# First modulation matrix in two column halves, with the first products of two strips between them, and the bias passes in parts

## The chip, the core and the metric

The kernel runs on one NeuronCore of a Trainium2 chip. The metric is device time in microseconds (us) for one execution of the whole program. The kernel before has a median of 1760.36 us over 3 runs (1759.49 to 1760.89).

## What is computed

A transformer stack on 256 tokens of width 1024: two layers of one kind, then two of another, all in float32. What the change touches is the first thing the first layer does: a modulation vector out of the condition, a modulated RMS norm, and a gated feed-forward block (FFN) of inner width 2816. The relative-position bias of the window attention, which comes later, is prepared in the same opening.

```
cond = silu(c)
mod = cond @ w_mod[l] + b_mod[l]            # 9 vectors of 1024: sh1, sc1, g1, ...
h = modulate(x, norm_g[l, 0], sh1, sc1)     # rms_norm(x) * g * (1 + sc1) + sh1
x = x + 0.5 * g1 * swiglu(h, w_ffn1_gu[l], w_ffn1_down[l])
...
bias[h, q, k] = rel_bias[bucket(pos_q - pos_k), h]   # window attention, masked where k > q
```

Each float32 product is made of three products in a reduced format: a "hi" part and a "lo" remainder of both operands, as hi*hi + lo*hi + hi*lo.

## The kernel before

**Weights.** A weight unit is 128 x 1024 float32, 512 KB. SyncE's queue loads units into a ring of 6 (`raw`); ScalarE makes the hi part of a unit (`hi_static`, L810), VectorE the lo part (`lo_static`, L1355), both into rings of 7. The queue reloads a ring slot when the lo part is done (`lo_done`). The first FFN has 11 strips of 256 inner columns. A strip is four gate/up units and two down units. The first three strips (0, 1, 2) have the tokens as the stationary operand (`gate_up`, `strip_unit`); from strip 3 on the weights are stationary (`turned_unit`). The gate/up sums of strip 0 lie in PSUM banks 2 and 3, those of strips 1 and 2 in banks 4 and 5 (`gu_banks`).

**The opening.** The first two modulation vectors, sh1 and sc1, are needed before any product can be made. Their matrix, 1024 x 2048, is loaded as 16 units (m0 to m15; m0 to m7 are all rows of the sc1 columns, m8 to m15 those of the sh1 columns) through SyncE's queue, into 4 arena tiles and the 6 ring slots, some of them twice (`mod_load` then waits for `mod_read`). TensorE multiplies each by the condition (`mod_unit`, L2222). VectorE turns the result into columns, `mod_store` (L1388 to L1390), the scale first and the shift in two pieces. Between the units TensorE makes four of the six bias passes (`bias_pass`, L2235, 16 small matmuls of 72 columns each) and transposes the normed x (`x_turn`, L2279). VectorE makes what a bias pass reads (`bias_reach`, L1397, 128 x 2048) and takes its result (`bias_take`, L1405, four reductions).

**Splitting x.** The transposed x comes as 8 groups: 4 pairs of 128-column chunks for each of 2 token halves. ScalarE and VectorE scale and shift them (`x_scaled`, L851 and L1472); ScalarE writes the hi part (`x_hi`, L860), VectorE the lo part (`x_low`, L1483). `opening_strip` (L2293, L2298) makes the products of strip 0, one unit at a time, each with two groups. Then comes the loop over strips: strip 1 with bias passes 4 and 5 in it, strip 2, and so on. After strip 0, VectorE computes `silu(gate) * up` in `gated` (L1679), TensorE transposes the product (`turn`, L2386), and the two are split for the down units.

**VectorE's modulation units.** All later modulation vectors are computed on VectorE (`mod_unit` there, L1368, one pass of 128 x 1024 each), from tiles that GpSimd's queue loads. In the first FFN there are 48, five or six for each strip from strip 2 on. VectorE's order in a turned strip is written out by hand: lo parts, modulation units, `half_sum` (L1690), lo parts, `half_made`, `half_lo`, and so on.

**The order** of the instructions of every engine is thus fixed in the text of the kernel; engines meet at semaphores. An engine that waits holds up all that stands behind it in its own order.

## Time and profile before

| | |
|---|---|
| median of 3 runs | 1760.36 us |
| profiled execution, its own time | 1760.84 us |
| its span in the trace | 1759.0 us |
| TensorE busy | 1733.1 us (99%) |
| VectorE busy | 1418.9 us (81%) |
| ScalarE busy | 1006.6 us (57%) |
| GpSimd busy | 186.0 us (11%) |
| HBM read | 438.38 MB, 250 GB/s over the span |

The span is 1.8 us shorter than the execution's own time, and that execution is 0.5 us above the median. Times in the rows are microseconds from the span's start. PE is TensorE, PEld its weight load, DVE VectorE, ACT ScalarE, POOL GpSimd, SP SyncE; a q behind the name is the engine's own sequencer. L with a number is a line of the kernel before. A float32 matmul that is not split shows as two instructions, so that one modulation unit on TensorE is x8.

### The profile page before, as it was taken

To read this page: it belongs to the slowest core of one execution; us is meant where nothing else is said; L and a number is where in the kernel's file an instruction comes from. 1 tells how busy PE (TensorE), PEld (TensorE's weight loads), DVE (VectorE), ACT (ScalarE), POOL (GpSimd) and SP (SyncE) were. 2 spreads that over 40 slices of the span, in tenths; PEclk is the share of its full clock that TensorE was granted. 3 is DMA by queue.
4 is the path that set the end of the run, shared out by engine and by line. 5 is a ranking of instruction groups with operands and counts; after the bars stand their busy time and mean duration, and the time that the engine had idled before them with its cause. 6 is when DMAs were issued, how large, how long until landed. Compare 5 with 4: busy or idle time off the path is not lost.

```text
span 1759.0 us, 24722 instructions
## 1 busy us (share of the span) xinstructions
PE 1733.1 (99%) x9178; PEld 1471.9 (84%) x9178; DVE 1418.9 (81%) x2185; ACT 1006.6 (57%) x1666; POOL 186.0 (11%) x382
## 2 busy tenths in 40 slices
PE   6999999999999999999999999999999999999998
PEld 3888888888888888988888888888888888888886
DVE  7899987898899888879888866579888876688565
ACT  4545577755475556877555644556455544465454
POOL 3021012111111111021110000001110000010000
PEclk9999999999999999999999999999999999999999
DMA  9999742698859985418898554458886484566551
GB/s 342 367 348 394 283 139 91 254 341 329 319 220 341 324 324 208 168 51 320 330 336 288 225 206 156 161 191 335 322 328 247 171 297 149 186 221 251 204 195 69
DMA packets 125144, 441.10 MB, mean 251 GB/s; under 512 B 15248, under 2 KB 18272, under 8 KB 124896
## 3 DMA queue, kind: packets, MB, share of 16 engines
q1 hardware_dynamic: 91024, 316.17, 48.9%
q0 software_dynamic: 33296, 120.12, 18.2%
q10 hardware_dynamic: 704, 3.23, 0.5%
q8 instruction: 73, 1.20, 0.3%
q14 instruction: 47, 0.39, 0.1%
HBM read 438.38 MB, written 1.09 MB: 250 GB/s over the span
## 4 chain that ended last, share of the span: by engine, by line
PE 95%; DVE 2%; DMA 1%; ACT 1%; issue 0%; SPq 0%; DVEq 0%; ACTq 0%
PE banks L2366 24%; PE banks L2167 15%; PE banks L2371 12%; PE banks L2145 12%; PE banks L2172 7%; PE banks L2150 6%; PE banks L2315 2%; PE banks L2319 2%; PE banks L2324 2%; PE banks L2135 1%; PE banks L2137 1%; PE banks L2136 1%; DMA weights_raw<-in_w_mod_first 1%; PE banks L2279 1%; PE banks L2604 1%; DVE weights_lo L1355 1%
## 5 line engine op out<-in xcount | busy, mean ns | idle before, releaser
L1355 DVE TENSOR_TENSOR weights_lo<-weights_raw,weights_hi 128x1024 fp32r<-128x1024 f32 (+2 forms) x584 | 685.7, 1200 | 67.8 <-ACT weights_hi L810 66.9
L810 ACT ACTIVATE weights_hi<-weights_raw 128x1024 fp32r<-128x1024 f32 (+2 forms) x584 | 584.5, 1035 | 69.3 <-DMA weights_raw<-in_w_in 22.0
L2366 PE MATMUL banks<-hT,weights_hi 128*128 128x512 f32 x1856 | 464.1, 392 | 0.0
L2366 PEld LDWEIGHTS banks<-hT,weights_hi 128*128 128x128 f32 x1856 | 337.3, 189 | 63.0
L2371 PEld LDWEIGHTS banks<-hT,weights_lo 128*128 128x128 f32 x1856 | 253.2, 190 | 18.1
L1368 DVE CUSTOM_DVE_ANT_0 arena<-arena,mod_acc,vectors 128x1024 f32<-128x1024 f32 x216 | 267.6, 1279 | 0.0
L2371 PE MATMUL banks<-hT,weights_lo 128*128 128x256 f32 x1856 | 258.8, 282 | 0.0
L1004 ACT ACTIVATE arena<-banks 128x512 f32<-128x512 f32 x116 | 69.5, 599 | 322.7 <-PE banks L2371 322.4
L2145 PE MATMUL banks<-weights_hi,hT 128*128 128x512 f32 (+2 forms) x896 | 218.2, 385 | 0.0
L2145 PEld LDWEIGHTS banks<-weights_hi,hT 128*128 128x128 f32 x896 | 165.6, 188 | 29.9
L1690 DVE TENSOR_TENSOR arena<-banks,arena 128x512 f32<-128x512 f32 x116 | 79.7, 687 | 109.0 <-ACT arena L1004 109.0
L2167 PE MATMUL banks<-weights_hi,actT_hi 128*128 128x512 f32 x520 | 140.7, 392 | 0.0
L2167 PE MATMUL banks<-weights_hi,actT_lo 128*128 128x512 f32 x520 | 139.3, 390 | 0.0
L2172 PE MATMUL banks<-weights_lo,actT_hi 128*128 128x512 f32 x520 | 139.0, 389 | 0.0
L2150 PE MATMUL banks<-weights_lo,hT 128*128 128x512 f32 (+2 forms) x448 | 116.9, 383 | 0.0
L2167 PEld LDWEIGHTS banks<-weights_hi,actT_lo 128*128 128x128 f32 x520 | 97.6, 188 | 21.1
L2172 PEld LDWEIGHTS banks<-weights_lo,actT_hi 128*128 128x128 f32 x520 | 97.6, 188 | 20.2
L2167 PEld LDWEIGHTS banks<-weights_hi,actT_hi 128*128 128x128 f32 x520 | 93.6, 189 | 16.2
L531 POOL DMA_DIRECT2D arena<-in_w_mod x128 | 67.7, 531 | 364.2 <-DVE mod_cols L1368 360.7
L2150 PEld LDWEIGHTS banks<-weights_lo,hT 128*128 128x128 f32 x448 | 83.7, 188 | 15.1
L1009 ACT ACTIVATE arena<-arena 128x256 f32<-128x256 f32 x116 | 48.1, 414 | 75.0 <-DVE arena L1690 74.8
L792 POOL TENSOR_TENSOR x<-x,arena 128x512 f32<-128x512 f32 x10 | 12.8, 1276 | 672.6 <-DVE arena L1513 672.6
(358 smaller groups left out, 1977.8 us busy)
## 6 DMA issues: line engine op xcount, KB each, us to landing
weights_raw<-in_w_ffn_gu SPq DMA_DIRECT2D x176, 512.0 KB, 4.8
arena<-in_w_mod POOLq DMA_DIRECT2D x128, 512.0 KB, 6.2
weights_raw<-in_w_in SPq DMA_DIRECT2D x104, 512.0 KB, 4.2
weights_raw<-in_w_ffn_down SPq DMA_DIRECT2D x88, 512.0 KB, 5.0
arena<-in_w_ada POOLq DMA_DIRECT2D x88, 512.0 KB, 5.6
weights_raw<-in_w_ffn_in SPq DMA_DIRECT2D x88, 512.0 KB, 4.1
weights_raw<-in_w_ffn_out SPq DMA_DIRECT2D x44, 512.0 KB, 4.3
weights_raw<-in_w_out SPq DMA_DIRECT2D x32, 512.0 KB, 3.9
```

Source lines behind the costliest of these rows:

```text
L531: eng.dma_start(mod_tile(m), mod_rows(m)).then_inc(S(mod_sem(m)), 16)
L810: nc.scalar.activation(whi[:, n % PARTS, 0:width], raw[:, slot, 0:width], ACT.Copy).then_inc(S("hi_done"), credit(n))
L1004: nc.scalar.activation(cross_t[:, j], half_banks(j)[:, :, 256:512], ACT.Copy).then_inc(S("half_by_act"), 1)
L1355: V.tensor_tensor(wlo[:, n % PARTS, 0:width], raw[:, n % RING, 0:width], whi[:, n % PARTS, 0:width].bitcast(F32), ALU.subtract).then_inc(S ...
L1368: V.tensor_tensor_reduce(modw[m % MOD_RING], modw[m % MOD_RING], cond_row, 1.0, vec[:, m:m + 1], ALU.mult, ALU.add, modc[:, m:m + 1])\
L1690: V.tensor_tensor(sum_t[:, j], half_banks(j)[:, :, 0:256], cross_t[:, j], ALU.add).then_inc(S("half_by_dve"), 1)
L2145: T.matmul(bank[banks[t]][:, 0:width], src[:, 2 * u + k, P * t:P * (t + 1)], whi[:, slot, k * width:(k + 1) * width], start=u == 0 and k = ...
L2150: ins = T.matmul(bank[banks[t]][:, 0:width], hi_[:, 2 * u + k, P * t:P * (t + 1)], wlo[:, slot, k * width:(k + 1) * width], start=False, s ...
L2167: T.matmul(bank[first_bank + 2 * t + h][:, :], src[:, c, P * t:P * (t + 1)], whi[:, slot, 512 * h:512 * (h + 1)], start=first and i == 0, ...
L2172: ins = T.matmul(bank[first_bank + 2 * t + h][:, :], hi_[:, c, P * t:P * (t + 1)], wlo[:, slot, 512 * h:512 * (h + 1)], start=False, stop= ...
L2366: T.matmul(half_banks(j)[:, kind, :], whi[:, n % PARTS, 256 * k + P * kind:256 * k + P * (kind + 1)], hx[:, :, 4 * q + k, :], start=q == 0 ...
L2371: ins = T.matmul(half_banks(j)[:, kind, 256:512], wlo[:, n % PARTS, 256 * k + P * kind:256 * k + P * (kind + 1)], hhi[:, 4 * q + k, :], st ...
```

## The change

1. **The matrix in halves.** The 16 units are laid out anew: m0 to m7 are all 1024 rows of the first 512 columns of both sh1 and sc1, m8 to m15 the same of the last 512. Every unit has a home of its own (6 ring slots, two tiles of `modacc`, six of `modw`, one arena tile, `gate_b`), so no load waits for a read. Some homes share a semaphore (`FIRST_SEMS`): a reader of m0, m1 or m2 waits for all three, one of m3, m4 or m5 for those three, and m8 with m9, m10 with m11, m12 with m13 in the same way.
2. **The queue.** SyncE's queue now carries m0 to m7, then weight units 0 and 1 (when m0 and m1 are read), m8, m9, unit 2, m10, m11, unit 3, m12 to m15, and units 4 to 7.
3. **The order of products.** The first eight weight units are, as (strip, row group): (0,0), (0,1), (1,0), (1,1), (0,2), (0,3), (1,2), (1,3). The first four need only the first half of the modulation and four of the eight groups of x. m8 to m15 are multiplied between them. The transposes of x come in two lots of 8. `silu` and `gated` of strip 0 come after unit 5 instead of unit 3, its `turn` after unit 6.
4. **`mod_store`** runs once for each half, and makes the scale columns too.
5. **Bias passes.** Three passes (1, 2 and 5) cover only the 64 query rows that are not masked; the other rows of `bias` are set to zero at the start. Passes 0 to 2 stand after m2, m4 and m5; passes 3 to 5 are made in nine parts of 6, 5 and 5 matmuls, in bank 7, between units 5 and 13, each taken by VectorE with one reduction (`bias_take_part`) before the next.
6. **GpSimd's queue** starts its loads for VectorE's modulation units after the hi part of unit 5 instead of unit 3.
7. Three pairs of semaphores are merged into one each (`uq_copied`, `up_copied`, `mix_ready`), with the counts adapted.

The core of the diff:

```diff
-FIRST_RING = 4
+FIRST_SEMS = (0, 0, 0, 3, 3, 3, 6, 7, 8, 8, 10, 10, 12, 12, 14, 15)
+FIRST_UNITS = ((0, 0), (0, 1), (1, 0), (1, 1), (0, 2), (0, 3), (1, 2), (1, 3))
...
-BIAS_AFTER = (2, 4, 8, 9)
-MOD_AHEAD = 12
-X_TURN_AFTER = (8, 12)
+BIAS_AFTER = (2, 4, 5)
+BIAS_ROWS = ((0, P), (64, P), (0, 64), (0, P), (0, P), (64, P))
+REACHED_AT = (0, 1, 0, 2, 3, 2)
+BIAS_PARTS = ((0, 6), (6, 11), (11, 16))
+BIAS_TAKEN = len(BIAS_AFTER) + 3 * len(BIAS_PARTS)
...
+            def first_weights(u):
+
+                b, k = FIRST_UNITS[u]
+                loaded = f"first_w_loaded{u}" if u < PREFETCH else f"w_loaded{u % RING // 2}"
+                if u < RING:
+                    sp.wait_ge(S("mod_read"), u + 1)
+                elif u == RING:
+                    sp.wait_ge(S("lo_done"), RING + 2)
+                sp.dma_start(raw[:, u % RING, :], phases[0][2]["gu"][b, k]).then_inc(S(loaded), 16)
+
+            first_units(0, 8)
+            first_weights(0)
+            first_weights(1)
+            first_units(8, 10)
+            first_weights(2)
+            first_units(10, 12)
+            first_weights(3)
+            first_units(12, 16)
+            for u in range(4, 8):
+                first_weights(u)
...
+                    if f == 0:
+                        pool.wait_ge(S("hi_done"), RING + 6)
...
+            def mod_store(half):
+
+                dve.wait_ge(S("mod_summed"), half + 1)
+                eye = con[:, C_EYE:C_EYE + 32].unsqueeze(1).broadcast_to([P, 8, 32])
+                then(V.tensor_tensor(modm, bank[sum_bank(half)][:, 0:256].rearrange("p (k j) -> p k j", j=32), eye, ALU.mult))
+                then(V.tensor_reduce(modr[:, :], modm, AX, ALU.add))
+                cols = slice(4 * half, 4 * half + 4)
+                at = [w[:, 0:16].rearrange("p (c k) -> p c k", c=2)[:, :, cols] for w in (modc, vec)]
+                then(V.tensor_tensor(at[0], modr[:, :].rearrange("p (c k) -> p c k", c=2), at[1], ALU.add))
+                g = phases[0][2]["g"] + 4 * half
+                V.scalar_tensor_tensor(sclA[:, cols], modc[:, 8 + 4 * half:12 + 4 * half], 1.0, vec[:, g:g + 4], ALU.add, ALU.mult)\
+                    .then_inc(S("mod_stored"), 1)
...
+                r0, r1 = BIAS_ROWS[q]
+                V.tensor_tensor(reached[REACHED_AT[q]][:, :, r0:r1], posf_q[:, q0 + r0:q0 + r1].unsqueeze(1).broadcast_to([P, 16, r1 - r0]),
+                                posf_k[:, kb, c0:c0 + 16].unsqueeze(2).broadcast_to([P, 16, r1 - r0]), ALU.is_ge).then_inc(S("reached"), 1)
...
+            def bias_take_part(i):
+
+                dve.wait_ge(S("bias_summed"), len(BIAS_AFTER) + i + 1)
+                bias_sums(3 + i // 3, 7, *BIAS_PARTS[i % 3]).then_inc(S("bias_taken"), 1)
...
+            x_stats(1, 0)
+            x_scale0(1)
             bias_take(0)
             bias_reach(2)
             bias_take(1)
-            x_stats(1, 0)
-            x_scale0(1)
-            bias_reach(3)
-            bias_take(2)
             x_stats(1, 1)
             x_scale1(1)
-            mod_store(1)
-            scale_cols(phases[0][2])
-            bias_take(3)
-            bias_reach(4)
-            mod_store(0, 0, 2)
+            bias_take(2)
+            scales[0] = 1
+            mod_store(0)
...
                 if phase[0] == 1:
-                    dve.wait_ge(S("mod_stored"), 2)
+                    dve.wait_ge(S("mod_stored"), 1)
                     x_scaled(a, 0, (0,), first=True)
-                    mod_store(0, 2, 8)
-                    dve.wait_ge(S("mod_stored"), 3)
                     x_low(0)
                     lo_static(n0, SLOT)
                     x_scaled(a, 2, first=True)
                     x_low(1)
-                    x_scaled(a, 3, first=True)
+                    x_scaled(a, 3, (0,), first=True)
                     lo_static(n0 + 1, SLOT)
                     x_low(2)
                     x_low(3)
                     lo_static(n0 + 2, SLOT)
+                    bias_reach(3)
+                    lo_static(n0 + 3, SLOT)
+                    mod_store(1)
+                    dve.wait_ge(S("mod_stored"), 2)
+                    x_scaled(a, 4, (0,), first=True)
                     x_low(4)
-                    x_scaled(a, 5, first=True)
-                    lo_static(n0 + 3, SLOT)
+                    x_scaled(a, 6, first=True)
                     x_low(5)
+                    lo_static(n0 + 4, SLOT)
+                    x_scaled(a, 7, (0,), first=True)
                     x_low(6)
                     x_low(7)
+                    lo_static(n0 + 5, SLOT)
                     x_split_done()
...
+                        c = n0 + 4
+                        units(c + 2, c + 3)
+                        bias_reach(4)
+                        gated(0)
+                        bias_take_part(0)
+                        units(c + 3, c + 4)
+                        act_lo(0)
+                        bias_take_part(1)
+                        units(c + 4, c + 6)
+                        bias_take_part(2)
+                        units(c + 6, c + 8)
+                        bias_take_part(3)
+                        gated(1)
+                        c, mods = n0 + 10, mod_slot(f, 2)
+                        dve.wait_ge(S("cond_row_ready"), 1)
+                        units(c + 2, c + 4)
+                        bias_take_part(4)
                         bias_reach(5)
+                        mod_units(mods[0:1])
+                        bias_take_part(5)
+                        mod_units(mods[1:2])
+                        act_lo(1)
+                        bias_take_part(6)
+                        mod_units(mods[2:3])
+                        units(c + 4, c + 5)
+                        bias_take_part(7)
+                        mod_units(mods[3:])
+                        units(c + 5, c + 6)
+                        bias_take_part(8)
                         units(c + 6, c + 8)
+                        gated(2)
+                        bias_mask(0, 3 * P)
...
+            def bias_part(i):
+
+                pe.wait_ge(S("reached"), 4 + i // 3)
+                pe.wait_ge(S("bias_taken"), len(BIAS_AFTER) + i)
+                bias_products(3 + i // 3, 7, *BIAS_PARTS[i % 3]).then_inc(S("bias_summed"), 1)
...
+            def opening_unit(n, banks, u):
+
+                slot = n % PARTS
+                pe.wait_ge(S("hi_done"), n + 1)
+                for src, sem in ((hhi, "hhi_done"), (hlo, "hlo_done")):
+                    for t in range(NT):
+                        pe.wait_ge(S(sem), tr[0] + 2 * u + t + 1)
+                        for c in range(2):
+                            T.matmul(bank[banks[t]][:, :], src[:, 2 * u + c, P * t:P * (t + 1)], whi[:, slot, 512 * c:512 * (c + 1)],
+                                     start=sem == "hhi_done" and u == 0 and c == 0, stop=False)
+                pe.wait_ge(S("lo_done"), n + 1)
+                for t in range(NT):
+                    for c in range(2):
+                        ins = T.matmul(bank[banks[t]][:, :], hhi[:, 2 * u + c, P * t:P * (t + 1)], wlo[:, slot, 512 * c:512 * (c + 1)],
+                                       start=False, stop=u == 3 and c == 1)
+                ins.then_inc(S("mm_done"), 1)
...
+            def opening(n):
+
+                strips = (gu_banks(0), gu_banks(1))
+                for m in range(8):
+                    if m == 7:
+                        x_turn(1, (0, 1), 1)
+                    mod_unit(m)
+                    if m in BIAS_AFTER:
+                        bias_pass(BIAS_AFTER.index(m))
+                    if m == 4:
+                        pe.wait_ge(S("const_loaded"), 16)
+                        x_turn(0, (0, 1), 1)
+                pe.wait_ge(S("bias_taken"), len(BIAS_AFTER))
+                keep_warm(WARM[0])
                 for u in range(4):
-                    slot = (n + u) % PARTS
-                    pe.wait_ge(S("hi_done"), n + u + 1)
-                    for src, sem in ((hhi, "hhi_done"), (hlo, "hlo_done")):
-                        for t in range(NT):
-                            if u == 0 and t == 1:
-                                pe.wait_ge(S("mod_stored"), 3)
-                            pe.wait_ge(S(sem), tr[0] + 2 * u + t + 1)
-                            for c in range(2):
-                                T.matmul(bank[banks[t]][:, :], src[:, 2 * u + c, P * t:P * (t + 1)], whi[:, slot, 512 * c:512 * (c + 1)],
-                                         start=sem == "hhi_done" and u == 0 and c == 0, stop=False)
-                    pe.wait_ge(S("lo_done"), n + u + 1)
-                    for t in range(NT):
-                        for c in range(2):
-                            ins = T.matmul(bank[banks[t]][:, :], hhi[:, 2 * u + c, P * t:P * (t + 1)], wlo[:, slot, 512 * c:512 * (c + 1)],
-                                           start=False, stop=u == 3 and c == 1)
-                    ins.then_inc(S("mm_done"), 1)
-                tr[0] += X_GROUPS
+                    b, k = FIRST_UNITS[u]
+                    opening_unit(n + u, strips[b], k)
+                    if u < 2:
+                        mod_unit(8 + 2 * u)
+                        mod_unit(9 + 2 * u)
+                    if u == 1:
+                        pe.wait_ge(S("scaled_by_dve"), 3)
+                        pe.wait_ge(S("scaled_by_act"), 3)
+                        x_turn(0, (2, 3), 1)
+                        x_turn(1, (2, 3), 1)
+                    if u == 2:
+                        for m in range(12, 16):
+                            mod_unit(m)
...
+                        if b == 1:
+                            for u in range(4, 8):
+                                s, k = FIRST_UNITS[u]
+                                opening_unit(n0 + u, gu_banks(s), k)
+                                if u == 6:
+                                    turn(0)
+                                if u > 4:
+                                    bias_part(u - 5)
+                            tr[0] += X_GROUPS
+                            down(c + 4, 0, 0, 1)
+                            bias_part(3)
+                            down(c + 4, 0, 1, 2)
+                            bias_part(4)
+                            continue
+                        pe.wait_ge(S("act_ready"), rows_made + b)
+                        gate_up(c, 0, 1)
+                        bias_part(5)
+                        gate_up(c, 1, 2)
                         turn(b - 1)
+                        bias_part(6)
                         gate_up(c, 2, 3)
-                        if f == 0 and b == 1:
-                            bias_pass(5)
-                            pe.wait_ge(S("const_loaded"), 32)
+                        bias_part(7)
                         gate_up(c, 3, 4)
-                        if f == 0 and b == 1:
-                            pe.wait_ge(S("bias_taken"), 6)
+                        bias_part(8)
                         down(c + 4, b - 1)
+                        pe.wait_ge(S("bias_taken"), BIAS_TAKEN)
...
-    laid["w_mod_first"] = np.roll(np.asarray(inputs["w_mod"])[0, :, 0:2 * D], D, axis=1)
+    laid["w_mod_first"] = np.asarray(inputs["w_mod"])[0, :, 0:2 * D].reshape(D, 2, 2, 512).transpose(2, 0, 1, 3).reshape(2, D, D)
```

## Rows read from the trace of the kernel before

**Rows 1.** The page: the chain that ended last, shares by engine.
```profile
PE 95%; DVE 2%; DMA 1%; ACT 1%; issue 0%; SPq 0%; DVEq 0%; ACTq 0%
```
**Rows 2.** Stages: busy us of PE, PEld, DVE, ACT, POOL; granted clock; DMA share; GB/s.
```profile
...
34.00:39.00 5.00, 4.55 (x13) 3.25 (x14) 5.00 (x11) 4.14 (x9) 0.00 (x0) 0.66 0.64 241
39.00:82.00 43.00, 43.00 (x222) 35.41 (x221) 37.98 (x51) 23.89 (x37) 6.58 (x12) 1.00 0.96 372
82.00:226.00 144.00, 143.25 (x755) 122.76 (x754) 140.50 (x204) 79.14 (x121) 24.77 (x49) 1.00 0.88 330
226.00:1759.00 1533.00, 1523.55 (x7977) 1300.81 (x7975) 1210.95 (x1865) 887.14 (x1478) 142.32 (x297) 1.00 0.65 238
...
```
**Rows 3.** The chain that ended last, opening: start, length, what.
```profile
...
5.67 14.74 DMA weights_raw<-in_w_mod_first
...
24.67 5.59 DMA weights_raw<-in_w_mod_first
...
```
**Rows 4.** TensorE's instructions in order of time, 0 to 95 us: start, length, what, idle before.
```profile
...
11.29 1.08 PE L2222 MATMUL banks<-arena,silu_cond 128*32 128x256 f32 x8 [0.20 <-DMA arena<-in_w_mod_first]
12.30 1.14 PE L2235 MATMUL banks<-arena 128*128 128x72 bf16 x16
...
25.30 1.50 PE L2222 MATMUL banks<-arena,silu_cond 128*32 128x256 f32 x24
27.08 1.09 PE L2279 MATMUL banks<-con,arena 128*128 128x128 f32 x8 [0.28 <-DVE window_bias L1405]
...
33.87 0.70 PE L2293 MATMUL banks<-weights_hi,hT 128*128 128x512 f32 x2 [1.78 <-ACT hT L860]
35.02 2.82 PE L2293 MATMUL banks<-weights_hi,hT 128*128 128x512 f32 x6 [0.45 <-ACT hT L860]
...
38.98 1.98 PE L2293 MATMUL banks<-weights_hi,hT 128*128 128x512 f32 x8
...
41.70 1.98 PE L2293 MATMUL banks<-weights_hi,hT 128*128 128x512 f32 x8
...
52.59 0.69 PE L2235 MATMUL banks<-arena 128*128 128x72 bf16 x16
53.12 0.63 PE L2386 MATMUL banks<-con,arena 128*128 128x128 f32 x4
...
81.94 1.98 PE L2366 MATMUL banks<-hT,weights_hi 128*128 128x512 f32 x8
...
```
**Rows 5.** VectorE's instructions in order of time, 0 to 226 us.
```profile
...
8.19 4.55 DVE L1397 TENSOR_TENSOR arena<-arena 128x2048 bf16<-128x2048 f32 x2
...
17.22 1.54 DVE L1405 TENSOR_REDUCE window_bias<-banks 128x96 f32<-128x288 f32 x4
...
23.35 0.15 DVE L1452 RECIPROCAL stat<-stat 128x1 f32<-128x1 f32 x1
...
24.07 0.41 DVE L1388 TENSOR_TENSOR arena<-banks,con 128x256 f32<-128x256 f32 x1
...
25.17 0.17 DVE L1603 SCALAR_TENSOR_TENSOR scale_cols<-mod_cols,vectors 128x8 f32<-128x8 f32 x1
...
66.99 1.28 DVE L1368 CUSTOM_DVE_ANT_0 arena<-arena,mod_acc,vectors 128x1024 f32<-128x1024 f32 x1
...
73.63 4.62 DVE L1355 TENSOR_TENSOR weights_lo<-weights_raw,weights_hi 128x1024 fp32r<-128x1024 f32 x4
78.17 0.74 DVE L1679 TENSOR_TENSOR arena<-arena,banks 128x256 f32<-128x256 f32 x2
...
85.98 0.69 DVE L1684 TENSOR_TENSOR actT_lo<-banks,actT_hi 128x512 fp32r<-128x512 f32 x1 [1.13 <-ACT actT_hi L997]
...
211.80 0.69 DVE L1690 TENSOR_TENSOR arena<-banks,arena 128x512 f32<-128x512 f32 x1 [0.20 <-ACT arena L1004]
...
```
**Rows 6.** ScalarE's instructions in order of time, 0 to 95 us.
```profile
...
31.88 1.06 ACT L810 ACTIVATE weights_hi<-weights_raw 128x1024 fp32r<-128x1024 f32 x1 [6.10 <-DMA weights_raw<-in_w_ffn_gu]
32.84 0.44 ACT L851 ACTIVATE arena<-banks,mod_cols,scale_cols 128x128 f32<-128x128 f32 x1
...
```

220 lines of the change are left out of this document (93 added, 127 removed).

## The prediction

> **What bounds the kernel now.** I read the page's chain first: TensorE holds 95% of the chain that ended last [rows 1]. The stages say where it is not busy: from 39 to 82 us it works 43.00 of 43 us, from 82 to 226 us, the rest of the first FFN, 143.25 of 144, and behind that 1523.55 of 1533 [rows 2]. So a microsecond saved in the opening is kept to the end, if no other engine holds it back. The opening's chain is loading: until 20.41 and again until 30.26 us TensorE's work waits for the first modulation matrix [rows 3], and the first product of the FFN starts at 33.87 [rows 4]. The row that matters as much is the other busy engine: VectorE works 140.50 of the 144 us up to the end of the first FFN [rows 2]. It has next to nothing to give, so TensorE can't run away from it there.
>
> My ledger is therefore in three parts: when the first product starts, when TensorE is through with strip 2 (its next instruction starts at 81.94 now [rows 4]), and where VectorE stands at that time (it starts `gated(2)` at 78.17 [rows 5]).
>
> **Step 1: the first product.** m0 to m2 now share a semaphore, so TensorE starts with m2, at 11.29 as now [rows 4]. Three units at the pace of that row (1.01 to the next) end at 14.4, bias pass 0 at 1.14 at 15.5. From here VectorE's order rules. One take is 1.54, of which the next instruction overlaps some 0.08 (four lo parts are 4.62 long and the next starts 4.54 after): 1.46. A reach is half of 4.55, so a half one 1.13; the reciprocal and the scaling of x take 0.72 (23.35 to 24.07) [rows 5]. Take, half reach, take, scaling, take: 15.6 + 1.46 + 1.13 + 1.46 + 0.72 + 1.46 = 21.9. TensorE meanwhile waits with pass 2 for the second take (19.7) and has pass 2, m6, four transposes and m7 left, half a us each: 21.9 as well, 22.1 with its drain. `mod_store` is 24.07 to 25.34, 1.27 [rows 5]: 23.4. ScalarE then needs a scaling and a hi part, 0.44 each by the row of the scaling [rows 6], and I give 0.1 for the crossings: the first product at 24.4, 9.5 us earlier than now. All loads that this needs are in by then: m8, the ninth unit, lands at 20.41 now [rows 3].
>
> **Step 2: TensorE from there to the end of strip 2.** Now it is 81.94 - 33.87 = 48.1 us: 16 weight units at 2.72 (38.98 to 41.70), 43.5; two bias passes at 0.53 (52.59 to 53.12); two turns, 0.4 each; and 2.7 of waiting and slow clock, nearly all in the first unit, which takes 5.11 [rows 4]. After the change it is: the same 43.5 and 0.8; eight modulation units moved behind the first product, at 0.5 (three in 1.50), 4.0; eight transposes, 1.0 [rows 4]; three bias passes instead of two, 1.6, and 0.3 for entering nine parts instead of three passes, an estimate. Then the waits, from the written orders. In unit 0 group 1's hi part comes 1.2 after group 0's (two scalings and a hi part) against 0.45 of products, 0.7; its lo part stands on VectorE behind the lo part of unit 0 (1.13) and two scalings, 0.5 more. At unit 4, ScalarE makes the hi part of the unit only behind groups 4 and 5: m15's product is ready at 38.9, `mod_store` 1.27, then 0.4, 0.35, 0.7, 0.35 and 1.06 [rows 6] give 43.1, and unit 3 is over at 41.5: 1.6. Units 5 and 10 and the end add 0.6. Waits 3.4. The sum is 54.6, the end 79.0: **2.9 us earlier**. Of the 9.5 us, 4.0 and 1.0 are work only moved, 0.8 is bias work, 0.7 more waits.
>
> **Step 3: VectorE.** Its cost falls by three half reaches (3.4 us), but its place is set by TensorE: it can't store the second half before m15's product. That is unit 0 (2.7 and 1.2), m8 and m9 (1.0), unit 1 (2.7), m10 and m11 (1.0), transposes (1.0), unit 2 (2.7), m12 to m15 (2.0) behind 24.4: 38.7, ready at 38.9. Until then VectorE has run dry: its work from 23.4 (four groups, four lo parts, a reach) ends near 33, more than 5 us idle. From 38.9 to `gated(2)` it has: store 1.3; eight passes over groups at a third of a us, 2.6; 14 lo parts at 1.13, 15.9; a reach and a half one, 3.4; two `gated` at 0.66, 1.3; two lo parts of products at 0.6, 1.2; nine parts of takes, 4.4 as three takes; five modulation units at 1.2, 6.0 [rows 5]; and waits of 3.4 (hi parts of groups 4 and 7 and of units 4 and 5, 2.1, and one for a turn like the 1.13 at 85.98). That is 39.5: `gated(2)` at 78.4, against 78.17 now. **VectorE gains nothing in the opening.**
>
> From there both orders are the same. VectorE's idle time in this stage is 144 - 140.5 = 3.5 us [rows 2]. 1.13 at 85.98 is a wait for ScalarE and, through it, for TensorE [rows 5], with 0.3 behind it; some 0.6 more, the 0.20 at 211.80 in it [rows 5], lies where VectorE has caught up with TensorE in the last strips; with TensorE nearly 3 us earlier these 2.0 us vanish. The other 1.5 are hops of the chain that ends the FFN and stay. So VectorE reaches the last strip 1.8 us earlier, and TensorE, 2.9 early from strip 3 on, waits about 1 us for the split of the last strip's product before its last matmuls. In between there is cover: VectorE takes a strip's sums well before TensorE comes back to their banks. The gain that is left: **1.9 us**. Behind the FFN all engines start together, and nothing else changes (the merged semaphores cost nothing: the same two signals, counted in one).
>
> **The clock.** From 34 to 39 us the granted clock is 0.66 [rows 2], part of the stretch at the 1.2 GHz level, after TensorE had waited 1.78 and 0.45 [rows 4]. Ten matmuls there take 35.02 to 38.98, 3.96 where twelve take 2.72 later: 1.7 us lost. The new order has waits of 1.0, 0.7 and 0.5 around unit 0 and 1.6 before unit 4. A fall at unit 0 delays TensorE and VectorE alike: gain 0.4. A fall at unit 4 overlaps waiting: gain about 1. Or none. I take **1.4 us** for the forecast, nearer to the case without, since the waits are shorter than the one before the fall.
>
> The Trainium skill ("TensorE: Matmul & The Clock Gate", section "Part 1: The HAM clock gate") says that the throttled clock is the default state and sustained activity releases it. By that rule the slow pace of the first units (1.01) would last longer when TensorE starts at 11.29 and not before, so that m3, m4 and pass 1 would take twice their time too. Two units and a pass at the slow rows end 0.5 us behind VectorE's half reach: the gain would be 0.5 less, inside the forecast. The recorded clock shows no low level in these first units, so the trace doesn't decide it.
>
> **Rivals.** *VectorE doesn't bind.* If its waits in step 3 are shorter (it only has 3.4 of them), TensorE's 2.9 come through: 1760.36 - 2.9 = 1757.5. If its waits in unit 0 and before unit 4 shrink too, more. For it speaks that the first unit now loses 2.4 with a slow clock in it; against it VectorE's 140.5 of 144. Chance 0.18, a third of it beyond 3.5 us.
> *Slower: the moved waits meet the slow clock twice.* Place: unit 0 and unit 4; price 1.7 and 1.1, with 0.5 in the first units, 3.3 against 1.9: 1761.8. It decides as soon as `gated(2)` starts more than 1.9 us behind 78.4. For it: the waits are written into the order. Chance 0.12.
> *The loads bind anyway, and the change doesn't do what it says.* m15 is now 20th in the queue. From the ninth (20.41) to the 16th (30.26) a unit took 1.41 [rows 3], so it lands at 35.9, before its product's turn at 38.2. With the queue 0.2 slower per unit the cover is gone, and each further 0.1 costs 1.1 us; 0.4 slower and the gain is used up: no change, 1760.4. DMA share is 0.96 from 39 to 82 us [rows 2]: little to spare. Chance 0.08.
> *Forecast* as above: 0.62.
>
> **Numbers.** The sum is made against the profiled execution, whose span of 1759.0 lies 1.8 below its own time 1760.84, itself 0.5 above the median; I take the gain off the median: 1760.36 - 1.4 = 1759.0. The range goes from the first rival with a little more (1757.2) to between no change and the slower one (1761.3); what is beyond is about 0.15. 0.2% is 3.5 us, about what a measurement of this kernel tells from no change: faster than that 0.08 (part of the first rival and an overlooked gain), slower 0.06 (half of the second), the same 0.86.
>
> **What would show it.** First product at 24 to 25; m15's product near 38.5; `gated(2)` within 1 us of 78.2; strip 3 starting near 79; VectorE without its wait at 86; a new wait of about 1 us on TensorE before the last matmuls of the first FFN, near 213. Wrong, if VectorE's place at strip 3 differs from now by over 1.5 us, if TensorE stalls in strips 3 to 9, or if the last stage (1533 us now) changes its length.

## The result and the profile of the changed kernel

The changed kernel is slower: 1762.72 us median of 20 runs (1761.91 to 1764.17) against 1760.49 (1759.49 to 1761.57) of the kernel before in the same runs, ratio 1.0014 [1.0008, 1.002]. I had predicted 1759.0 with a range to 1761.3; the time lies above it, though within the 0.2% that I had called no difference. The profiled execution took 1764.04 us (span 1762.2), 1.3 above its median; the one of before was 0.35 above 1760.49. So the two traces lie 3.2 us apart where the medians lie 2.2.

First the page's chain, then the stages of the changed kernel (columns as in [rows 2]):

```profile
PE 88%; DVE 9%; DMA 1%; ACT 1%; issue 0%; SPq 0%; DVEq 0%; ACTq 0%
```

```profile
34.00:39.00 5.00, 5.00 (x48) 3.71 (x50) 0.00 (x0) 0.00 (x0) 0.00 (x0) 1.00 1.03 420
39.00:82.00 43.00, 39.75 (x218) 30.20 (x207) 36.46 (x53) 22.69 (x35) 5.78 (x11) 1.00 0.78 291
82.00:226.00 144.00, 142.92 (x752) 121.94 (x751) 142.49 (x204) 76.80 (x114) 22.29 (x42) 1.00 0.90 342
226.00:1762.00 1536.00, 1526.28 (x7988) 1302.84 (x7986) 1212.53 (x1869) 889.30 (x1484) 144.94 (x304) 1.00 0.65 237
```

VectorE's share of the chain went from 2 to 9% [rows 1]. There is no slow clock from 34 to 39 us. From 39 to 82 us TensorE, which had no gap there [rows 2], stands still for 3.3 us; from 82 to 226 VectorE has 1.5 us of idle time left where it had 3.5.

TensorE in order of time (start, length, what, idle before):

```profile
24.66 0.71 PE L2363 MATMUL banks<-weights_hi,hT 128*128 128x512 f32 x2 [1.31 <-ACT hT L877]
...
29.82 2.11 PE L2363 MATMUL banks<-weights_hi,hT 128*128 128x512 f32 x8
31.77 1.07 PE L2368 MATMUL banks<-weights_lo,hT 128*128 128x512 f32 x4
32.77 1.07 PE L2284 MATMUL banks<-arena,silu_cond 128*32 128x256 f32 x16
...
43.93 2.14 PE L2363 MATMUL banks<-weights_hi,hT 128*128 128x512 f32 x8 [1.50 <-ACT weights_hi L829]
...
49.84 0.37 PE L2292 MATMUL banks<-arena 128*128 128x72 bf16 x6
50.05 2.09 PE L2363 MATMUL banks<-weights_hi,hT 128*128 128x512 f32 x8
...
52.91 0.60 PE L2473 MATMUL banks<-con,arena 128*128 128x128 f32 x4
...
62.98 2.11 PE L2207 MATMUL banks<-weights_hi,hT 128*128 128x512 f32 x8 [0.22 <-DVE arena L1723]
...
67.52 0.32 PE L2292 MATMUL banks<-arena 128*128 128x72 bf16 x5 [1.53 <-DVE window_bias L1438]
...
83.65 2.06 PE L2453 MATMUL banks<-hT,weights_hi 128*128 128x512 f32 x8
```

The first product comes at 24.66 instead of 33.87 [rows 4], 9.2 us earlier, as forecast (24.4). (In two later traces of the kernel before with a small edit, e4 and e11, it comes at 32.76 and 32.74, where the last unit of the matrix is multiplied 0.8 us earlier; against those the gain is 8.1.) The first product of strip 3 comes at 83.65 instead of 81.94: all of it is used up, and 1.7 more. Two things are to be seen on the way. The waits: 1.50 as forecast, and 1.53 for a bias take, which was not. And the units: 29.82 to 32.77 is 2.95, 50.05 to 52.91 is 2.86, where a unit of the kernel before took 2.72 [rows 4].

And one thing at the end: strip 3's first product waits for the result of `gated(2)` (`pe.wait_ge(S("act_ready"), rows_made + b)`). In the kernel before, `gated(2)` starts 3.8 us ahead of strip 3 and nobody waits. In the changed kernel and in all its versions below strip 3 starts 0.85 or 0.86 us behind the start of `gated(2)`: VectorE sets this start. Here TensorE's own last unit is over at 83.43, so its wait is only 0.2 us.

VectorE, and ScalarE's two waits for loads:

```profile
39.55 0.42 DVE L1414 TENSOR_TENSOR arena<-banks,con 128x256 f32<-128x256 f32 x1 [5.77 <-PE banks L2284]
...
59.38 2.36 DVE L1379 TENSOR_TENSOR weights_lo<-weights_raw,weights_hi 128x1024 fp32r<-128x1024 f32 x2 [1.37 <-ACT weights_hi L829]
...
64.57 2.36 DVE L1379 TENSOR_TENSOR weights_lo<-weights_raw,weights_hi 128x1024 fp32r<-128x1024 f32 x2 [1.65 <-ACT weights_hi L829]
66.84 0.53 DVE L1438 TENSOR_REDUCE window_bias<-banks 128x120 f32<-128x360 f32 x1
67.28 1.22 DVE L1431 TENSOR_TENSOR arena<-arena 128x1024 bf16<-128x1024 f32 x1
...
82.80 0.75 DVE L1723 TENSOR_TENSOR arena<-arena,banks 128x256 f32<-128x256 f32 x2
...
214.25 0.69 DVE L1734 TENSOR_TENSOR arena<-banks,arena 128x512 f32<-128x512 f32 x1 [0.20 <-ACT arena L1023]
```

```profile
58.29 2.01 ACT L829 ACTIVATE weights_hi<-weights_raw 128x1024 fp32r<-128x1024 f32 x2 [2.26 <-DMA weights_raw<-in_w_ffn_gu]
...
63.40 2.01 ACT L829 ACTIVATE weights_hi<-weights_raw 128x1024 fp32r<-128x1024 f32 x2 [2.56 <-DMA weights_raw<-in_w_ffn_gu]
```

`gated(2)` starts at 82.80, 4.6 us later than before [rows 5] and 4.4 later than forecast. The last `half_sum` of the first FFN is at 214.25 against 211.80 [rows 5], 2.45 later. ScalarE's waits for units 10 to 13, and VectorE's behind them, are not new. The trace of the kernel before has them at the same places:

```profile
58.39 2.01 ACT L810 ACTIVATE weights_hi<-weights_raw 128x1024 fp32r<-128x1024 f32 x2 [2.11 <-DMA weights_raw<-in_w_ffn_gu]
...
63.62 2.01 ACT L810 ACTIVATE weights_hi<-weights_raw 128x1024 fp32r<-128x1024 f32 x2 [2.68 <-DMA weights_raw<-in_w_ffn_gu]
```

```profile
64.71 2.36 DVE L1355 TENSOR_TENSOR weights_lo<-weights_raw,weights_hi 128x1024 fp32r<-128x1024 f32 x2 [2.20 <-ACT weights_hi L810]
```

Units 10 to 13 are ready for ScalarE 0.1 to 0.2 us earlier than before, although the first product comes 9.2 us earlier. The loads of these units, for which ScalarE waits at 58.29 and 63.40, share the DMA engines with six modulation loads of GpSimd. The issues of both queues, and the stages from 40 us on:

```profile
47.23 3.13 POOL L535 DMA_DIRECT2D arena<-in_w_mod  x6 [16.21 <-ACT weights_hi L829]
```

```profile
48.20 6.55 SPq L574 DMA_DIRECT2D weights_raw<-in_w_ffn_gu  x4
```

```profile
40.00:44.00 4.00, 2.50 (x12) 1.75 (x10) 2.75 (x9) 3.06 (x7) 0.00 (x0) 1.00 0.58 198
44.00:48.00 4.00, 4.00 (x16) 2.96 (x17) 3.26 (x5) 2.84 (x5) 0.77 (x2) 1.00 0.35 140
...
56.00:60.00 4.00, 4.00 (x28) 3.00 (x27) 2.63 (x4) 1.74 (x3) 0.00 (x0) 1.00 1.04 422
```

The DMA engines are half idle from 40 to 48 us (shares 0.58 and 0.35; in the kernel before 0.94 and 1.00) and then full (1.04 from 56 us), with ten units asked for within 8 us.

### The profile page after: what moved, and what is told of

It is laid out like the page before. It is cut to its first block, busy times and chain, and to the rows that moved or that the text cites. A ratio compares the mean times of both kernels' runs of the same rounds, so it can differ in the third digit from the quotient of the medians.

```text
span 1762.2 us, 24721 instructions
## 1 busy us (share of the span) xinstructions
PE 1733.7 (98%) x9178; PEld 1470.2 (83%) x9178; DVE 1417.0 (80%) x2184; ACT 1005.8 (57%) x1665; POOL 183.1 (10%) x382
## 4 chain that ended last, share of the span: by engine, by line
PE 88%; DVE 9%; DMA 1%; ACT 1%; issue 0%; SPq 0%; DVEq 0%; ACTq 0%
PE banks L2453 21%; PE banks L2229 13%; PE banks L2458 11%; PE banks L2207 11%; PE banks L2234 7%; PE banks L2212 5%; DVE weights_lo L1379 4%; DVE arena L1396 3%; PE banks L2413 2%; PE banks L2417 2%; PE banks L2422 2%; PE banks L2197 2%; PE banks L2199 2%; PE banks L2198 2%; PE banks L2352 1%; DVE arena L1734 1%
## 5 line engine op out<-in xcount | busy, mean ns | idle before, releaser
L2207 PE MATMUL banks<-weights_hi,hT 128*128 128x512 f32 (+2 forms) x864 | 210.5, 386 | 0.2 <-DVE arena L1723 0.2
L2207 PEld LDWEIGHTS banks<-weights_hi,hT 128*128 128x128 f32 x864 | 159.5, 188 | 29.0 <-DVE arena L1723 0.3
L2212 PE MATMUL banks<-weights_lo,hT 128*128 128x512 f32 (+2 forms) x432 | 112.7, 382 | 0.0
L811 POOL TENSOR_TENSOR x<-x,arena 128x512 f32<-128x512 f32 x10 | 13.2, 1319 | 672.4 <-DVE arena L1556 672.4
```

The source lines that it names most:

```text
L2207: T.matmul(bank[banks[t]][:, 0:width], src[:, 2 * u + k, P * t:P * (t + 1)], whi[:, slot, k * width:(k + 1) * width], start=u == 0 and k = ...
L2212: ins = T.matmul(bank[banks[t]][:, 0:width], hi_[:, 2 * u + k, P * t:P * (t + 1)], wlo[:, slot, k * width:(k + 1) * width], start=False, s ...
```

## The experiments

Thirteen runs followed: the changed kernel once more (a1) and twelve kernels with an edit. The table gives five places of each profiled execution (us from the start of the span) and the median of its runs; "gap" is the last `half_sum` less `gated(2)`. Medians are to be read against the kernel before in the same runs, at 1760.49 for after and 1760.05 to 1760.15 for the others; each row has 11 runs, but after 20, e5 5 and e10 one. The intervals of the versions overlap (e5's only just), so the medians don't rank them; the readings below rest on the places in one trace of each. Where the table compares places, mind that the first modulation unit's product started anywhere from 10.56 to 12.36 us in the changed kernel's family: places are best counted from the first product. That too has a trap. In e1, e5, e10 and e12 the granted clock fell in unit 0 (0.80, 0.72, 0.76 and 0.66 from 23 to 28 us, 1.00 in the other eight traces of the family), and the unit took 5.17 to 5.43 us instead of 4.16: 1.0 to 1.3 us that I don't put down to the edits: those of e1, e5 and e10 lie behind this unit, and e8 has e12's opening without the fall.

| kernel | first product | `gated(2)` | strip 3 | last `half_sum` | gap | median | ratio to before |
|---|---|---|---|---|---|---|---|
| before | 33.87 | 78.17 | 81.94 | 211.80 | 133.63 | | |
| after | 24.66 | 82.80 | 83.65 | 214.25 | 131.45 | 1762.72 | 1.0014 [1.0008, 1.002] |
| a1 after again | 25.55 | 82.88 | 83.73 | 214.35 | 131.47 | 1763.13 | 1.0016 [1.0008, 1.0025] |
| e1 loads early | 24.03 | 81.39 | 82.24 | 212.84 | 131.45 | 1762.39 | 1.0011 [1.0002, 1.002] |
| e2 reach early | 24.11 | 81.38 | 82.23 | 213.48 | 132.10 | 1763.5 | 1.0018 [1.0009, 1.0027] |
| e3 both | 23.52 | 81.22 | 82.07 | 212.68 | 131.46 | 1761.91 | 1.0009 [1.0, 1.0018] |
| e6 loads late | 23.54 | 79.93 | 80.78 | 211.39 | 131.46 | 1761.85 | 1.0009 [1.0001, 1.0018] |
| e4 before + reach | 32.76 | 77.42 | 81.04 | 211.61 | 134.19 | 1760.77 | 1.0003 [0.9994, 1.0012] |
| e5 after + reach | 23.85 | 82.21 | 83.06 | 216.03 | 133.82 | 1766.66 | 1.0037 [1.0024, 1.0049] |
| e7 between | 24.05 | 80.15 | 81.00 | 212.72 | 132.57 | 1761.97 | 1.0009 [1.0, 1.0018] |
| e8 pass 0 first | 22.80 | 78.90 | 79.75 | 211.29 | 132.39 | 1760.54 | 1.0005 [0.9996, 1.0014] |
| e9 no parts | 23.64 | 78.02 | 78.87 | 210.11 | 132.09 | 1760.48 | 1.0001 [0.9992, 1.001] |
| e10 units together | 23.99 | 80.89 | 81.74 | 212.49 | 131.60 | (1762.17) | |
| e11 before, merged | 32.74 | 77.00 | 80.86 | 210.71 | 133.71 | 1760.4 | 1.0001 [0.9992, 1.0011] |
| e12 pass 0, loads 9 | 23.04 | 80.27 | 81.13 | 211.78 | 131.51 | 1761.16 | 1.0006 [0.9997, 1.0015] |

### What delays VectorE: four places of the loads and the reach

e1 takes the wait of part 6 away, e6 raises it, e2 moves a reach into VectorE's idle time, e3 is e1 and e2 together.

```diff
 e1, e3:
-                    if f == 0:
-                        pool.wait_ge(S("hi_done"), RING + 6)
 e6:
-                        pool.wait_ge(S("hi_done"), RING + 6)
+                        pool.wait_ge(S("hi_done"), RING + 13)
 e2, e3 (bias_reach(4) gone from in front of gated(0)):
                     lo_static(n0 + 3, SLOT)
+                    bias_reach(4)
                     mod_store(1)
```

> The changed kernel with GpSimd's first six modulation loads no longer held back behind the hi part of unit 5. They can start once m15's product is made, near 39.6 us, where the queues stand half idle (DMA share 0.58 and 0.35 from 40 to 48 us in the changed kernel). Theory A (the loads): units 10 to 13 arrive late because the six loads start at 47.2, just before unit 10's at 48.2. Then unit 10's hi part starts near 56 instead of 58.3, VectorE loses its waits of 1.37 and 1.65 us, gated(2) starts near 80 instead of 82.8, and the time is 2.5 to 3 us below the changed kernel's, 1759.7 to 1760.2. Theory B (unit 10 is late because its own load is issued late, at 48.2, behind the lo part of unit 5): its landing hardly moves, gated(2) stays near 82.5, and the time stays at 1762.5. Theory C (VectorE isn't what binds): gated(2) moves, the time doesn't.

> The changed kernel with the reach of bias pass 4 moved from behind the lo part of unit 6 into the 5.8 us in which VectorE stands idle before m15's product. Theory A: the lo parts of units 7 to 9 come 2.2 us earlier, but VectorE then waits that much longer for units 10 and 12, so gated(2) moves by under 0.7 us and the time by under 0.7. Theory B (VectorE's own work sets its place, the loads don't): gated(2) 2.2 us earlier, the time 2.2 us lower, 1760.5.

> Both edits. Theory A: with the loads early there is no wait left behind which the moved reach could hide, so the two add up: gated(2) near 78 us, VectorE 4.5 to 5 us ahead of the changed kernel, and TensorE's own order binds again: strip 3 starts near 81.5, and the time is 1759.5 to 1760.3, 0 to 1 us below the kernel before. If VectorE still bound, it would be 1757.9. Theory B: 1760.5, as the moved reach alone.

> The changed kernel with GpSimd's six modulation loads held back further, until the hi part of unit 12, so that units 10 and 11 have the queues to themselves. Theory A in its narrow form (the six loads and unit 10's share the queues): units 10 to 13 land at 53 to 57 us and VectorE doesn't wait for them; but the modulation units, needed from 68 us, land at 65 to 68, just in time or a little late, so that gated(2) starts at 80 to 81.5. Time 1760 to 1761.5. Theory B (late issue): unit 10 still lands near 58 and the time is 1762.7 or more.

None gives back the 4.4 us. e1 was expected near 80 and 1759.7 to 1760.2 and came at 81.39 and 1762.39; e3 was expected near 78 and 1759.5 to 1760.3 and came at 81.22 and 1761.91: both missed. e2's `gated(2)`, counted as below, moved by 0.1 to 0.9 us, near its Theory A; its median rose by 0.8. e6 came near its forecast (79.93 for 80 to 81.5, 1761.85 for 1760 to 1761.5). Counted from the first product, `gated(2)` comes at 58.1 (after) and 57.3 (a1), at 57.4, 57.3 and 57.7 in e1, e2 and e3, and at 56.4 in e6. Counted from `mod_store` behind m15's product (39.55 in after), past the slow clock in e1's unit 0, it is 43.3 and 42.4, then 41.2, 42.4 and 42.8, and 41.5 in e6: e1 gives as much as e6. In e1 ScalarE waits 1.20 for units 10 and 11 and not at all for 12 and 13; VectorE gets 1.18 of it back as a wait for the turn of strip 1, at 70.36. In e2 the reach is gone from the full stretch, and in its place VectorE waits 1.14 and 1.27 us for the silu and the turn of strip 0; its wait for units 12 and 13 stays (1.98, a1 1.96). In e3 ScalarE still waits 0.59 and 2.73 for units 10 to 13: the six loads start at 38.69, but one takes 12.2 us to land (median), and the DMA share is 1.01 to 1.03 from 44 to 56 us. Why e3 keeps this wait and e1 loses it is not shown. Of the four only e6, where the six loads start at 58.87, has no wait for units 10 to 13 at all. It has another instead (VectorE, e6):

```profile
67.70 1.28 DVE L1396 CUSTOM_DVE_ANT_0 arena<-arena,mod_acc,vectors 128x1024 f32<-128x1024 f32 x1 [1.64 <-DMA arena<-in_w_mod]
```

So the meeting of the two queues is what makes ScalarE and VectorE wait at 58 to 65 us, and it is worth 0.9 to 2.0 us at `gated(2)`, not 4.4. The Trainium skill ("DMA: Bandwidth & Descriptors", section "Queues, rings and completion order") says that each DMA engine takes turns between the queues that have work for it; ScalarE's waits with and without the six loads agree with that.

### Does VectorE bind?

```diff
 e4 (before), e5 (after): behind gated(2), result unused
+  then(V.tensor_tensor(reached[3], posf_q[:, 0:P]..., posf_k[:, 0, 0:16]..., ALU.is_ge))
```

> The changed kernel unaltered, beside the kernel before and the other kernels of this call, as the base that they are read against. Every theory: about 2.2 us above the kernel before. The later runs of the family differed in when TensorE's first product of the modulation starts (10.56 to 11.47 us); if that alone spreads the times, this execution's place at gated(2) minus its first start stays 71.3 us, as it was (82.80 less 11.47).

> The kernel before with one more bias reach (2.2 us on VectorE, its result is not used) between gated(2) and the mask. Theory A (VectorE binds the first FFN in the changed kernel only, in the kernel before it stands just behind the bound with about 2 us of idle time that can vanish): 0.2 to 0.5 us slower. Theory B (VectorE binds in both kernels alike): 2.2 us slower. Theory C (VectorE binds in neither): no change.

> The changed kernel with the same extra reach at the same place. Theories A and B (VectorE binds the first FFN): 2.0 to 2.3 us slower than the changed kernel, and the last half_sum 2.2 us later. Theory C (TensorE's own order sets the end and VectorE has cover): under 0.5 us slower.

The extra reach took 2.28 us. In the changed kernel the gap grew by 2.35, all of it; in the kernel before by 0.56. The medians say the same, more coarsely: 3.5 us over a1 and 0.7 over before (within its interval of no change). Both are above what the gap gives; e5 has only five runs, and its profiled execution (1765.51 against a1's 1763.88) shows 1.6. Theory A holds: VectorE binds in the changed kernel, and stands some 1.7 us (2.28 less 0.56) in front of the bound in the kernel before; 0.31 of the 0.56 is a wait for a modulation load at 131.45 that its own trace doesn't have. The table's gap shows the same wall: 131.45 to 131.60 in the seven executions where VectorE waits for nothing on the way but the last 0.20 (after, a1, e1, e3, e6, e10, e12), 133.63 before. TensorE's wait before the last matmuls of the FFN, which I had looked for, is not in the changed kernel's trace: there TensorE itself starts strip 3 late, behind `gated(2)`. It stands in e4, and in e7 further down, where a load has put VectorE 1 us behind (e4, then e7):

```profile
213.81 0.47 PE L2197 MATMUL banks<-weights_hi,actT_hi 128*128 128x512 f32 x1 [0.35 <-ACT actT_hi L1014]
```

```profile
214.92 0.47 PE L2256 MATMUL banks<-weights_hi,actT_hi 128*128 128x512 f32 x1 [1.06 <-ACT actT_hi L1033]
```

a1's `gated(2)` is 70.5 us behind the first modulation unit, after's 71.3: the start of that unit explains most of the spread, not all. (a1 waits 0.8 us less for units 10 to 13, at the same kernel.)

### Behind VectorE: TensorE's changes of kind

```diff
 e7 (with bias_reach(4) early as in e2; base of e8 to e10, e12):
-                        pool.wait_ge(S("hi_done"), RING + 6)
+                        pool.wait_ge(S("hi_done"), RING + 11)
 e9: e7 without bias_part(0 to 8), bias_take_part(0 to 8), bias_reach(3 to 5); their columns of bias set to zero
 e10:
-                    if u < 2:
-                        mod_unit(8 + 2 * u)
-                        mod_unit(9 + 2 * u)
+                    if u == 1:
+                        for m in range(8, 12):
+                            mod_unit(m)
```

> The changed kernel with bias reach 4 moved into VectorE's idle time before m15's product, and GpSimd's six loads begun after the hi part of unit 10 instead of unit 5: late enough to keep clear of units 10 to 13, and earlier than after unit 12, where VectorE waited 1.64 us for them. Theory A (reach and loads are what put VectorE behind): gated(2) near 76.5 to 78, strip 3 near 80.5 with TensorE then the later of the two, the first FFN ends 1 to 1.5 us before that of the kernel before, and the time is 0.5 to 1.5 us below the kernel before. Rival (the nine takes and the switching between kinds of matmul on TensorE are what costs): gated(2) not below 79, and the time at or above the kernel before.

> The last version (reach 4 early, loads after the hi part of unit 10) without bias passes 3 to 5: their nine parts on TensorE, nine takes and three reaches on VectorE are left out, and the bias columns that they make are zero. My price of the parts on TensorE was 1.6 us for the matmuls and 0.3 for entering them. If that is right, strip 3 starts 1.9 to 2.2 us earlier than in the last version (81.00 less the difference in starts). If each change of the kind of matmul costs the unit behind it 0.1 to 0.2 us, as the units' lengths of 2.86 instead of 2.72 in the last trace suggest, it starts 3.0 to 3.8 earlier, and the units 5 to 15 are back at 2.72. VectorE has 8 us less, so TensorE sets the end of the first FFN: the time falls by what strip 3 does, unless the loads from 100 to 190 us bind (then by less than 2).

> One look. The last version with m8 to m11 multiplied together behind unit 1, instead of two behind unit 0 and two behind unit 1: one block of another kind of matmul less between the weight units, the same work. By the price of a change of kind (0.15 to 0.25 us), unit 1 takes 2.72 instead of 2.95 and the products behind come 0.2 us earlier counted from the first product. By my prediction's accounting (work only moved) nothing changes.

e7 is the case of its rival: `gated(2)` at 80.15, not 76.5 to 78. No load holds VectorE any more before 132 us; it waits for what TensorE makes (the silu of strip 0, two turns), and then once for a load:

```profile
49.83 0.75 DVE L1724 TENSOR_TENSOR arena<-arena,banks 128x256 f32<-128x256 f32 x2 [1.13 <-ACT arena L1011]
...
53.55 0.69 DVE L1729 TENSOR_TENSOR actT_lo<-banks,actT_hi 128x512 fp32r<-128x512 f32 x1 [1.27 <-ACT actT_hi L1016]
...
69.11 0.69 DVE L1729 TENSOR_TENSOR actT_lo<-banks,actT_hi 128x512 fp32r<-128x512 f32 x1 [1.58 <-ACT actT_hi L1016]
...
132.59 1.28 DVE L1396 CUSTOM_DVE_ANT_0 arena<-arena,mod_acc,vectors 128x1024 f32<-128x1024 f32 x1 [1.03 <-DMA arena<-in_w_mod]
```

e9 leaves the parts out, and with them the neighbours' surcharge. Its TensorE:

```profile
60.15 1.98 PE L2196 MATMUL banks<-weights_hi,hT 128*128 128x512 f32 x8
61.97 1.07 PE L2201 MATMUL banks<-weights_lo,hT 128*128 128x512 f32 x4
62.87 1.98 PE L2196 MATMUL banks<-weights_hi,hT 128*128 128x512 f32 x8
```

The unit is back at 2.72 (2.83 where a turn stands in front of it). From the first product to the end of strip 2's last unit e7 needs 56.7 us (80.77 less 24.05), e9 53.3 (76.95 less 23.64): the nine parts cost 3.4 us, within the 3.0 to 3.8 expected; the waits in the two stretches are the same. Their own blocks are 1.9 of that, 1.2 lie in the units beside them and 0.3 in the two turns, for which I had put 0.3 in all. e10, expected 0.2 us earlier from the first product on, can't be read from there, because its unit 0 has the slow clock; behind it, it agrees in sum: from unit 1's start to unit 2's it takes 5.56 us (29.19 to 34.75), where e7 takes 4.80 (29.21 to 34.01) and 1.00 for the two units ahead, 0.24 more in e7. Unit 1 is only down to 2.85, not the 2.72 expected; the rest is in the block of 32:

```profile
29.19 2.01 PE L2363 MATMUL banks<-weights_hi,hT 128*128 128x512 f32 x8
31.04 1.07 PE L2368 MATMUL banks<-weights_lo,hT 128*128 128x512 f32 x4
32.04 1.93 PE L2284 MATMUL banks<-arena,silu_cond 128*32 128x256 f32 x32
```

But e9's TensorE then stands 1.7 us before strip 3, until `gated(2)` is made, and its time is still that of the kernel before, with 6 us less on VectorE behind m15's product (the takes 5.0, a half reach 1.2) and 3.4 less on TensorE. ScalarE's rows name the third wall, and VectorE waits 2.94 at 65.71 for a modulation load:

```profile
70.52 2.01 ACT L829 ACTIVATE weights_hi<-weights_raw 128x1024 fp32r<-128x1024 f32 x2 [1.79 <-DMA weights_raw<-in_w_ffn_gu]
...
75.64 2.01 ACT L829 ACTIVATE weights_hi<-weights_raw 128x1024 fp32r<-128x1024 f32 x2 [2.33 <-DMA weights_raw<-in_w_ffn_gu]
```

The DMA share from 60 to 82 us is 1.03 in e9 (1.02 in e7, 0.79 in the changed kernel): in this stretch the loads bind e9.

### Pass 0 first, and where the loads start

In the profiled executions of the changed kernel and its versions up to here VectorE waits 1.6 to 2.9 us for bias pass 0, which stands behind three loads (the changed kernel's own trace has the 1.6; the expectation below gives 2.0 as the least).

```diff
 e8 (e7 and), e12 (e8 with RING + 9):
                 strips = (gu_banks(0), gu_banks(1))
+                bias_pass(0)
                 for m in range(8):
 ...
-                    if m in BIAS_AFTER:
-                        bias_pass(BIAS_AFTER.index(m))
+                    if m in BIAS_AFTER[:2]:
+                        bias_pass(1 + BIAS_AFTER.index(m))
```

> The last version (reach 4 early, GpSimd's loads after the hi part of unit 10), and now bias pass 0 stands ahead of m0 to m2 instead of behind them, passes 1 and 2 behind m2 and m4. In every execution of the changed kernel so far VectorE waited 2.0 to 2.9 us for pass 0, while TensorE waited for the three units. Theory: the first product comes 11 to 11.5 us behind the first modulation unit instead of 13.2, and strip 3 and gated(2) 1.5 to 2 us earlier than in the last version; the time is 1 to 1.5 us below the kernel before. Rival (the loads: the DMA share is 0.97 to 1.03 from 100 to 190 us, and VectorE waited 1.03 us at 132.6 for a modulation load): the wait there grows by what the opening gives, the last half_sum stays at 212 to 213, and the time is within 0.5 us of the last version.

> The version with bias pass 0 first and reach 4 early, with GpSimd's six loads begun after the hi part of unit 8 instead of unit 10, some 2.5 us earlier, since the DMA engines stand idle nearly half of the time from 40 to 52 us. If the modulation load for which VectorE waited 0.82 us at 131 is late because all loads behind 52 us are, that wait shrinks or goes, and the last half_sum comes up to 0.8 us earlier: 1759.8 to 1760.5, level with the kernel before. If the loads of that stage are set by the DMA engines' share from 100 us on (0.97 and more), the wait stays, and the time is that of the version with pass 0 first, 0.5 us above the kernel before; if the six loads meet units 10 to 13, ScalarE waits for those again.

e8's first product comes 11.5 us behind the first modulation unit (22.80 less 11.28) instead of 13.2, as expected, strip 3 at 79.75, and the median is 1.4 below e7's (each against the kernel before in its runs; the intervals overlap). But it is 0.5 above the kernel before, not 1 to 1.5 below: VectorE waits 0.82 at 131.14 for a modulation load. In e12 that wait is gone, and ScalarE has 1.17 at 72.28 and 1.23 at 89.25 for weight loads instead; strip 3 is 1.1 us further from the first product, which is a slow clock in unit 0 (granted 0.66 from 23 to 28 us, 1.00 in e8; six matmuls at 24.09 take 2.74, where e8's six take 2.26 with a wait of 0.33 among them). From `mod_store` behind m15's product to `gated(2)` both need 41.2 us. The two don't decide which start is better; neither beats the kernel before.

### The end of the program

```diff
 e11, the kernel before with part 7 alone, for example:
-                    pe.wait_ge(S("uq_copied0"), m + 1)
-                    pe.wait_ge(S("uq_copied1"), m + 1)
+                    pe.wait_ge(S("uq_copied"), 2 * (m + 1))
```

> The kernel before with part 7 of the change alone: the three pairs of semaphores merged. In all profiled executions of the changed kernel and its versions the span ends 4.7 to 4.8 us behind the issue of the last output DMA, in the two of the kernel before and its version 3.6 to 3.7 us, and from the last half_sum of the first FFN to the span's end it is 0.5 us longer. If the merged semaphores cause that, this kernel shows the longer end and is 0.5 us slower; if they cost nothing, as I predicted, its end is 3.6 to 3.7 us and its time that of the kernel before.

ScalarE's last rows of e11; its span ends at 1758.4:

```profile
1752.50 0.72 ACT L1335 ACTIVATE arena<-arena,stat 128x512 f32<-128x512 f32 x1 [0.27 <-DVE stat L1450]
1753.26 0.35 ACTq L1336 DMA_DIRECT2D out<-arena  x1
```

From the end of the last issue (1753.61) to the end of the span it is 4.8 us, as in the whole changed family (4.7 to 4.8), against 3.6 in the trace of before (its last issue starts at 1755.02 and is 0.35 long) and 3.7 in e4. Against that, from the last `half_sum` to the last scaling it is 1541.8 instead of 1542.5 and 1542.6. Both come with the merged semaphores. Together they are 0.4 us; the medians of e11 and before (1760.4 and 1760.15) can't tell that from nothing. It is one execution against two there, and thirteen with the longer end. What the engines do in that extra microsecond, the trace doesn't show.

## Why the prediction was wrong

**Step 1 was right.** First product 24.66 against 24.4. m3 and m4 kept the slow pace of the first units (15.26 to 17.12), pass 1 did not (0.66), at a granted clock of 1.00: the lateness that I had priced at 0.5 didn't come. The clock did not fall in the profiled execution, a case that I had allowed for; it did in unit 0 of four of the family's twelve (e12: 0.66 granted from 23 to 28 us, part of it at the 1.2 GHz level, behind waits of 1.31 and 0.35), and cost 1.0 to 1.3. My price of 1.7 was too high: unit 0 of the kernel before takes 5.11 with the fall [rows 4] and 4.11 in e4, whose clock is 1.00, so the fall costs 1.0.

**Step 2 failed in the price of work, above all in "0.3 for entering nine parts instead of three passes".** The ledger was 54.6 and measured 59.0 (24.66 to 83.65). The waits on it (0.34, 0.35, 1.50, 0.22, 1.53, and 0.2 for `gated(2)` at the end) are 4.2 against 3.4. The other 3.6 us are work, 54.8 for 51.2: the nine parts cost 3.4 (e9) for the 1.9 that I had put down, 1.5 more; unit 0 took 3.5 without its waits (m8 starts at 28.82), 0.8 more; units 1 to 5, beside modulation units, transposes and a wait (2.95 at 29.82), 1.1 more. I took them all at 2.72. The rows to see it by were there, in the kernel before, 2.84 for the unit behind a pass and a turn; I had read only the undisturbed unit [rows 4]:

```profile
53.51 2.09 PE L2145 MATMUL banks<-weights_hi,hT 128*128 128x512 f32 x8
55.44 1.08 PE L2150 MATMUL banks<-weights_lo,hT 128*128 128x512 f32 x4
56.35 0.69 PE L2235 MATMUL banks<-arena 128*128 128x72 bf16 x16
```

**Step 3 failed in VectorE's place: "`gated(2)` at 78.4" was 82.80.** Of the 4.4 us, 0.65 is m15's product (39.55 for 38.9), 1.1 is work (37.2 busy for 36.1), 2.6 are waits (6.0 for 3.4). Half of the extra work is the nine takes, 5.0 us for 4.4. The waits that my 3.4 left out are the 1.37 and 1.65 for units 10 to 13, and a wait for them of 2.20 was to be read in the kernel before, at 64.71: I added up VectorE's work and its waits for hi parts and a turn, and put the loads at nothing. I had placed the rival *the loads bind anyway* at m15, where nothing was waited for. It binds 20 us later: units 10 to 13 are ready no more than 0.2 us earlier than in the kernel before, with DMA engines that were half idle from 40 to 48 us. That parts 3 and 6 make this idle stretch is argued from the written orders; that the six loads of GpSimd make the wait is shown by e6, which gains 0.9 to 1.7 without them. e7 then shows TensorE's step 2 as the next thing late, and e9 the loads again.

**The relation behind it held.** I gave VectorE's idle time that can vanish as 2.0 us; the gap fell by 2.2, and VectorE waits neither at 86 us nor anywhere up to the last strip. With `gated(2)` 4.6 later the last `half_sum` should by this come 2.6 later, and came 2.45. e5 and e4 confirm the wall, and e4 its distance to 0.3 us. What the ledger lacked is the tie the other way: strip 3 can't start before `gated(2)` is made, so VectorE's 78.4 alone would have put it at 79.25 (0.85 behind), not 79.0. So *VectorE doesn't bind* is refuted. The slower rival was right in sign and in its deciding point (`gated(2)` more than 1.9 behind 78.4), and wrong in its mechanism: no clock fell.

**"The merged semaphores cost nothing" was off by 0.4 us** in the profiles (e11).

In sum, by the traces: 2.45 at the end of the first FFN and 0.75 behind it, of which 0.4 are the merged semaphores, make the 3.2 between the spans. The profiled execution of after was one of the slowest of its runs. What of the 2.2 between the medians lies in the first FFN is therefore only bounded: a1 and after both show 2.5 against the one trace of the kernel before, and e4 and e11 put that kernel 0.9 to 1.1 us earlier at strip 3 than its own trace did.

## What to carry to other kernels

Where three resources stand within two microseconds of each other, an earlier start is no gain until all three have room: price each one's ledger to the same place, loads included, beginning with the waits for loads that the old trace already has. Look for stretches where a reordering leaves the DMA engines idle and then asks for everything at once. Price small blocks that are put between large ones with their neighbours: compare the length of a unit beside such a block with one that stands alone. And fill an engine's idle time before adding work to its full stretch; here one pass more to take (three of the nine parts) and a reach moved from the opening into the stretch that sets the end, though e2, which moved the reach back, won at most 0.9 us by it, since other waits took its place.
